# Stick-breaking attention: pairs of heads, worked inside the key and value loops, with fp32r cumulative sums

## What is computed

```python
def _sb_block(q_blk, k, v, q_pos):
    t_len = k.shape[2]
    k_pos = jnp.arange(t_len)
    z = jnp.einsum('bhqd,bhkd->bhqk', q_blk, k).astype(jnp.float32) * (SB_HEAD_DIM ** -0.5)
    causal = k_pos[None, :] < q_pos[:, None]
    log_keep = jnp.where(causal, -jax.nn.softplus(z), 0.0)
    after = lax.cumsum(log_keep, axis=3, reverse=True) - log_keep
    w = jnp.where(causal, jnp.exp(jax.nn.log_sigmoid(z) + after), 0.0)
    return jnp.einsum('bhqk,bhkd->bhqd', w.astype(v.dtype), v)

def stick_breaking_mixer(x, w_qkv, w_o):
    qkv = (x @ w_qkv).reshape(b, t_len, 3, SB_HEADS, SB_HEAD_DIM).transpose(2, 0, 3, 1, 4)
    q, k, v = qkv[0], qkv[1], qkv[2]
    ...
    return o @ w_o
```

## Time and profile before

| | |
|---|---|
| median of 3 runs | 1375.29 us (1373.15 to 1376.83) |
| span of the profiled execution | 1373.0 us (the lowest run, 1373.15, is next to it; the median lies 2.3 us above it) |
| PE busy | 1300.8 us, 95% |
| DVE busy | 851.3 us, 62% |
| ACT busy | 667.8 us, 49% |
| POOL busy | 36.4 us, 3% |
| mean granted clock of PE | 0.977 |
| key units | until 717.0 us |
| scores of heads 0 to 2 | 717.0 to 719.2 us |
| value units | 719.2 to 752.9 us |
| loop over heads | 752.9 to 818.7 us |

### The profile page before, as it was taken

One profiled execution on the slowest core, in us unless ns is written; L12 is line 12 of the kernel. 1 busy time (PEld: TensorE's weight loads), 2 busy tenths in 40 slices (PEclk: granted clock), 3 DMA queues, 4 the chain that ended last, 5 costly groups with the idle time before them and its releaser, 6 DMA issues.

```text
span 1373.0 us, 26931 instructions
## 1 busy us (share of the span) xinstructions
PE 1300.8 (95%) x10012; PEld 1251.6 (91%) x10012; DVE 851.3 (62%) x1246; ACT 667.8 (49%) x1015; POOL 36.4 (3%) x58
## 2 busy tenths in 40 slices
PE   5989999999998999999899999999999478999997
PEld 5989789999997999999899779999999478999997
DVE  3897675887555777754554536665446586666443
ACT  4453436646344666644343545565443455565331
POOL 1001210100000000000000000000000000000000
PEclk9999999999999999999999999999999688999999
DMA  4445333565443555555253104555554234455551
GB/s 165 139 153 170 108 105 106 160 214 168 138 138 116 161 185 184 185 190 185 82 170 107 31 1 152 169 171 181 171 177 128 79 113 146 153 172 179 171 177 51
DMA packets 56754, 197.44 MB, mean 144 GB/s; under 512 B 7136, under 2 KB 9440, under 8 KB 56560
## 3 DMA queue, kind: packets, MB, share of 16 engines
q1 hardware_dynamic: 54144, 194.01, 43.8%
q10 hardware_dynamic: 2544, 2.51, 0.6%
HBM read 195.45 MB, written 1.05 MB: 143 GB/s over the span
## 4 chain that ended last, share of the span: by engine, by line
PE 86%; DVE 9%; ACT 2%; issue 2%; DMA 1%; DVEq 0%; SPq 0%; ACTq 0%
PE acc L363 23%; PE acc L365 22%; PE acc L364 22%; PE mix L418 3%; DVE wlo L1132 2%; PE acc L401 2%; PE acc L402 2%; PE acc L403 2%; DVE xc L1320 1%; PE mix L481 1%; DVE uu L1596 1%; ACT whi L796 1%; PE mix L694 1%; PE mix L421 1%; DMA raw<-w 1%
## 5 line engine op out<-in xcount | busy, mean ns | idle before, releaser
L796 ACT ACTIVATE whi<-raw 128x1024 fp32r<-128x1024 f32 x368 | 388.1, 1058 | 516.2 <-PE acc L365 459.8
L1132 DVE TENSOR_TENSOR wlo<-raw,whi 128x1024 fp32r<-128x1024 f32 x368 | 449.5, 1223 | 245.6 <-ACT whi L796 245.3
L363 PE MATMUL acc<-xh,whi 128*128 128x256 f32 (+1 forms) x1664 | 481.4, 289 | 19.1 <-DVE xl L1139 14.9
L365 PE MATMUL acc<-xh,wlo 128*128 128x256 f32 (+1 forms) x1664 | 477.4, 287 | 0.0
L364 PE MATMUL acc<-xl,whi 128*128 128x256 f32 (+1 forms) x1664 | 477.0, 287 | 0.0
L363 PEld LDWEIGHTS acc<-xh,whi 128*128 128x128 f32 x1664 | 317.5, 191 | 23.6 <-DVE wlo L1132 20.2
L365 PEld LDWEIGHTS acc<-xh,wlo 128*128 128x128 f32 x1664 | 317.7, 191 | 0.0
L364 PEld LDWEIGHTS acc<-xl,whi 128*128 128x128 f32 x1664 | 316.7, 190 | 0.2
L365 PE MATMUL acc<-hh,wlo 128*128 128x272 f32 (+1 forms) x688 | 196.8, 286 | 0.0
L363 PE MATMUL acc<-hh,whi 128*128 128x272 f32 (+1 forms) x688 | 196.8, 286 | 0.0
L364 PE MATMUL acc<-hl,whi 128*128 128x272 f32 (+1 forms) x688 | 196.7, 286 | 0.0
(11 more groups left out here) (320 smaller groups left out, 1530.7 us busy)
## 6 DMA issues: line engine op xcount, KB each, us to landing
raw<-w SPq DMA_DIRECT2D x368, 512.0 KB, 3.5
hT<-xT ACTq DMA_DIRECT2D x1, 1024.0 KB, 10.3
mem<-memT ACTq DMA_DIRECT2D x1, 1024.0 KB, 5.4
out<-hT SPq DMA_DIRECT2D x8, 128.0 KB, 2.0
xdt<-wsmall ACTq DMA_DIRECT2D x1, 192.0 KB, 10.1
pr<-par ACTq DMA_DIRECT2D x1, 114.0 KB, 10.0
hT<-metaT ACTq DMA_DIRECT2D x1, 64.0 KB, 10.8
bcn<-wa ACTq DMA_DIRECT2D x1, 32.0 KB, 9.6
```

The costliest lines, as they stand in the source:

```text
L363: nc.tensor.matmul(dst, whi[:, slot, n, :], rh, start=first, stop=False)
L365: return nc.tensor.matmul(dst, wlo[:, slot, n, :], rh, start=False, stop=last)
L796: act.activation(whi[:, j, :, :].rearrange("p k c -> p (k c)"), raw[:, j, :], ACT.Copy)\
L1132: dve.tensor_tensor(wlo[:, j, :, :].rearrange("p k c -> p (k c)"), raw[:, j, :], whi[:, j, :, :].rearrange("p k c -> p (k c)").bitcast(F32 ...
```

## The change

- Heads go in pairs, `PAIRS` = 8, and all four `mix` banks hold scores, two pairs in turn. PE's stream is one loop over m = 0 to 10: `sb_after(m-3)`, then key unit m (m < 8) or value token pair m-8, then `sb_scores(m-1)`. Then `sb_out` of pairs 0 to 3, the last value token pair, `sb_out` of pairs 4 to 7, and `project("so")`.
- `sb_scores(p)` issues the three strips of both heads in turn, so that matmuls on rows 0 to 63 and on rows 64 to 127 alternate, then adds the causal mask in the bank: three bf16 matmuls per head, identity times `cmask` (0 and -1e30), of 128, 128 and 16 columns. `nmask` and `bmask` and their making on POOL are gone.
- The softplus: DVE sets the sign bit of the scores out of PSUM (`soft_abs`, in place of ACT's Abs and the scale -1), ACT does Exp and Ln, DVE adds max(z, 0) (`soft_sum`). ACT copies it into fp32r (`soft_hi`), DVE takes the rest (`soft_lo`); the multiplication by the mask is gone.
- `sb_after(p)` takes the sum over `softh` and then over `softl`, with `ntri` and `nones` (fp32r copies of tiles that now hold -1): 12 fp32r matmuls per head of the same sizes as the six before.
- ACT exponentiates straight out of PSUM into `wT`, which has a buffer for each of the 16 heads; DVE's min and mask step is gone.
- `sb_out(p)` alternates between the two heads of a pair (64 stationary columns each, PSUM partitions 0 to 63 and 64 to 127).
- At the program's start POOL makes `cmask`, `ntri` and `nones` besides the other constants.

On PE before, in the loop over heads (the sums of head 1, the output of head 0, the beginning of the scores of head 4): `lk` is the masked softplus, `tri` and `ones` the stationary tiles.

```diff
...
+        sp = sb("sp", [P, 2, ZC], stack=s4)
+        spt = sb("spt", [P, 2, ZC], stack=s4)
+        softh = sb("softh", [P, 4, ZC], F32R, stack=s4)
+        softl = sb("softl", [P, 4, ZC], F32R, stack=s4)
+        wT = sb("wT", [P, SBH, ZC], stack=s4)
...
-        zbank = [mix[:, 0, :], mix[:, 1, :], mix[:, 3, :], acc[:, 0, :]]
-        obank = [mix[:, 2, :], acc[:, 1, :]]
...
             pool.affine_select(out=bigm[:, :], in_=bigm[:, :], compare_op=ALU.is_ge, fill=BIG, base=0,
                                pattern=[[1, P]], channel_multiplier=-1).then_inc(consts, 1)
+            pool.affine_select(out=cmask[:, :], in_=cmask[:, :], compare_op=ALU.is_gt, fill=-BIG, base=0,
+                               pattern=[[1, P]], channel_multiplier=-1).then_inc(consts, 1)
+            pool.wait_ge(consts, CONSTS - 2)
+            for tile, exact in ((tri, ntri), (ones, nones)):
+                pool.tensor_copy(exact[:, :], tile[:, :]).then_inc(consts, 1)
...
-            project("sk", xh, xl, T2)
...
+            add = dict(start=False, skip_group_check=True)
+            def sb_scores(p):
+                pe.wait_ge(evacuated[p % 4], (OUTS["sk"] + p) // 4 + 1)
+                if p == 0:
+                    pe.wait_ge(sbmask, 1)
+                if p == 1:
+                    pe.wait_ge(misc_free, R["st_sb"] + 1)
+                if p >= 2:
+                    pe.wait_ge(wT_ready, 2 * p - 2)
+                both = [(64 * i, mix[:, 2 * (p % 2) + i, :]) for i in range(2)]
                 for t in range(3):
...
+                    for po, z in both:
+                        nc.tensor.matmul(z[:, at_c[t]:at_c[t] + T2 - at_q[t]], skT[po:po + 64, p, P * t:P * t + P],
+                                         sqT[po:po + 64, p, at_q[t]:T2], start=t == 0, stop=t == 2)
+                for po, z in both:
+                    nc.tensor.matmul(z[:, 0:P], identb[:, :], cmask[:, :], stop=False, **add)
+                    nc.tensor.matmul(z[:, T2:T2 + P], identb[:, :], cmask[:, :], stop=False, **add)
+                    nc.tensor.matmul(z[:, 2 * T2 - P:ZC], identb[:, :], cmask[:, 0:META], stop=True, **add)\
+                        .then_inc(head_ready, 1)
+            def sb_after(p):
+                for h in (2 * p, 2 * p + 1):
+                    z = mix[:, 2 * (p % 2) + h % 2, :]
+                    pe.wait_ge(softl_ready, h + 1)
+                    for n, part in enumerate((softh, softl)):
+                        l = part[:, h % 4, :]
+                        nc.tensor.matmul(z[:, 0:T2], ntri[:, :], l[:, 0:T2], stop=False, **add)
+                        nc.tensor.matmul(z[:, P:T2], nones[:, :], l[:, T2:2 * T2 - P], stop=False, **add)
+                        nc.tensor.matmul(z[:, 2 * P:T2], nones[0:META, :], l[0:META, 2 * T2 - P:ZC], stop=False, **add)
+                        nc.tensor.matmul(z[:, T2:2 * T2 - P], ntri[:, :], l[:, T2:2 * T2 - P], stop=False, **add)
+                        nc.tensor.matmul(z[:, T2 + P:2 * T2 - P], nones[0:META, :], l[0:META, 2 * T2 - P:ZC],
+                                         stop=False, **add)
+                        last = nc.tensor.matmul(z[:, 2 * T2 - P:ZC], ntri[0:META, :], l[0:META, 2 * T2 - P:ZC],
+                                                stop=n == 1, **add)
+                    last.then_inc(tri_ready, 1)
+            def sb_out(p):
+                if p == 0:
+                    pe.wait_ge(wT_ready, SBH)
+                if p >= 4:
+                    pe.wait_ge(yl_ready, 32 + p - 3)
+                for j in (0, 1):
+                    pe.wait_ge(evacuated[2 * (p // 2 % 2) + j], OUTS["sv"] // 4 + p // 4 + 1)
+                at_k = ((0, P, 0, T2), (P, P, T2, 2 * T2 - P), (2 * P, META, 2 * T2 - P, ZC))
+                for t, (q0, n, lo, hi) in enumerate(at_k):
+                    for h in (2 * p, 2 * p + 1):
+                        po = 64 * (h % 2)
+                        last = nc.tensor.matmul(mix[po:po + 64, p % 4, q0:T2], sv[0:n, t, 64 * h:64 * h + 64],
+                                                wT[0:n, h, lo:hi], start=t == 0, stop=t == 2)
+                last.then_inc(pv_done, 1)
+            for m in range(PAIRS + 3):
+                if m >= 3:
+                    sb_after(m - 3)
+                if m < PAIRS:
+                    unit("sk", m, m % 4, xh, xl, T2)
+                else:
+                    token_pair("sv", 2 * (m - PAIRS), xh, xl, tiles2)
+                if 1 <= m <= PAIRS:
+                    sb_scores(m - 1)
             for p in range(4):
...
+                sb_out(p)
+            token_pair("sv", 6, xh, xl, tiles2)
+            for p in range(4, PAIRS):
+                sb_out(p)
             project("so", yh, yl, T2, (yl_ready, 32))
...
-            units_loop("sk")
             HB = SSD_HEADS + XH
             exp_ln_tables()
...
+            def soft_terms(p):
+                for h in (2 * p, 2 * p + 1):
+                    t = sp[:, h % 2, :]
+                    act.wait_ge(sb_abs, h + 1)
+                    act.activation(t, t, ACT.Exp).then_inc(sb_act, 1)
+                    act.wait_ge(sb_act, 2 * h + 1)
+                    act.activation(t, t, ACT.Ln, bias=1.0).then_inc(sb_act, 1)
+            def soft_hi(h):
+                act.wait_ge(soft_ready, h + 1)
+                if h >= 4:
+                    act.wait_ge(tri_ready, h - 3)
+                act.activation(softh[:, h % 4, :], spt[:, h % 2, :], ACT.Copy).then_inc(softh_ready, 1)
+            def weights(h):
+                act.wait_ge(tri_ready, h + 1)
+                act.activation(wT[:, h, :], mix[:, h % 4, 0:ZC], ACT.Exp).then_inc(wT_ready, 1)
             def pair_out(p):
...
+                act.wait_ge(pv_done, p + 1)
+                act.activation(yh[:, p, :], mix[:, p % 4, 0:T2], ACT.Copy).then_inc(yh_ready, 1)
+            for m in range(PAIRS + 3):
+                p, q = m - 2, m - 3
+                if 0 <= p < PAIRS:
+                    soft_terms(p)
+                    soft_hi(2 * p)
+                if q >= 0:
+                    weights(2 * q)
+                if 0 <= p < PAIRS:
+                    soft_hi(2 * p + 1)
+                if q >= 0:
+                    weights(2 * q + 1)
+                if m < PAIRS:
+                    split_hi(UNITS["sk"][0] + m + 4)
+                else:
+                    split_hi(UNITS["sv"][0] + 2 * (m - PAIRS) + 4)
+                    split_hi(UNITS["sv"][0] + 2 * (m - PAIRS) + 5)
+            for p in range(4):
+                pair_out(p)
+            split_hi(UNITS["sv"][0] + 10)
+            split_hi(UNITS["sv"][0] + 11)
+            for p in range(4, PAIRS):
+                pair_out(p)
             units_loop("so", after_residual("so", "mlp0", T2))
...
-            units_loop("sk", scaled(skT, T2))
             HB = SSD_HEADS + XH
...
+            def soft_abs(h):
+                dve.wait_ge(head_ready, HB + h + 1)
+                dve.tensor_scalar(sp[:, h % 2, :].bitcast(U32), mix[:, h % 4, 0:ZC].bitcast(U32), SIGN, None,
+                                  ALU.bitwise_or).then_inc(sb_abs, 1)
+            def soft_sum(h):
+                dve.wait_ge(sb_act, 2 * h + 2)
+                dve.scalar_tensor_tensor(out=spt[:, h % 2, :], in0=mix[:, h % 4, 0:ZC], scalar=0.0,
+                                         in1=sp[:, h % 2, :], op0=ALU.max, op1=ALU.add).then_inc(soft_ready, 1)
+            def soft_lo(h):
+                dve.wait_ge(softh_ready, h + 1)
+                dve.tensor_tensor(softl[:, h % 4, :], spt[:, h % 2, :], softh[:, h % 4, :].bitcast(F32), ALU.subtract)\
+                    .then_inc(softl_ready, 1)
             def pair_lo(p):
                 dve.wait_ge(yh_ready, 32 + p + 1)
-                dve.tensor_tensor(yl[:, p, :], obank[p % 2][:, 0:T2], yh[:, p, :].bitcast(F32), ALU.subtract)\
+                dve.tensor_tensor(yl[:, p, :], mix[:, p % 4, 0:T2], yh[:, p, :].bitcast(F32), ALU.subtract)\
                     .then_inc(yl_ready, 1)
...
+            def values(m):
+                dve.wait_ge(unit_done, UNITS["sv"][0] + 2 * m + 2)
+                token_scaled(sv, 2 * m, (P, P, META))
+                split_lo(UNITS["sv"][0] + 2 * m + 4)
+                split_lo(UNITS["sv"][0] + 2 * m + 5)
+            for m in range(PAIRS + 3):
+                p = m - 2
+                if 0 <= p < PAIRS:
+                    for step in (soft_abs, soft_sum, soft_lo):
+                        step(2 * p)
+                        step(2 * p + 1)
+                if m < PAIRS:
+                    dve.wait_ge(unit_done, UNITS["sk"][0] + m + 1)
+                    dve.tensor_tensor(skT[:, m, 0:T2], acc[:, m % 4, 0:T2], rstd[:, :], ALU.mult)\
+                        .then_inc(evacuated[m % 4], 1)
+                    split_lo(UNITS["sk"][0] + m + 4)
+                else:
+                    values(m - PAIRS)
             for p in range(4):
...
+                pair_lo(p)
+            values(3)
+            for p in range(4, PAIRS):
+                pair_lo(p)
```

(16 more changed lines are left out.)

114 lines of the change are left out of this document (8 added, 106 removed).

## The result

The changed kernel takes **1381.93 us** (median of 4 runs, 1379.99 to 1382.92) against 1374.22 us for the kernel before (4 runs, 1372.31 to 1376.83): ratio 1.0052, 95% interval 1.0038 to 1.0067. The forecast was 1366.8 with a range of 1361 to 1381. The kernel is slower by 7.7 us where 8.5 us less was forecast. In the profiled execution (1379.99 us) the span is 1378.2 us against 1373.0, and the mean granted clock of PE is 0.963 against 0.977.

The account below looks back on a forecast made before the run. PE was taken to bound the kernel, the attention costing 68.0 us of it. Terms +2.6 - 6.4 + 2.9 - 8.7 + 1.1 = -8.5 us took 1375.3 to 1366.8 us, range 1361 to 1381.

Parts of the forecast that it names:

- A clock below 1.00 there: Sign that would prove the forecast wrong: PE's granted clock under 1.00 between the last query matmul and `so`; no chance given.
- Sums: Softplus sums on PE, one fp32r pass over high and low parts: 2.38 us a head against 2.21, +2.6 us.
- that rival: Narrow fp32r matmuls in the sums are dear: +12.8 us (1379.6), with double loads +22 (1389); chance 0.24.
- Scores: Scores on PE, two heads side by side in row halves: 1.03 us a pair, 9.0 against 15.4, -6.4 us.
- Masks: Causal masks, new on PE as bf16 matmuls: 0.36 us a pair with the uncovered load, 8 times, +2.9 us.
- Outputs: Attention outputs on PE, two heads of a pair side by side: 1.07 us a pair, 8.6 against 17.0, -8.7 us.
- Start: Pipeline's start: PE waits once for the softplus chain before the first sum, +1.1 us.
- At no cost: POOL's constants and removed masks, `split_lo` behind the softplus steps on DVE, SP's queue: claimed to add nothing.

Follow-up runs that it names:

- the first experiment: The changed kernel with its sums in plain float32 over the softplus itself, without high and low parts: 1364.8 us, ratio 0.9938.

## Why the prediction was wrong

**The step that failed** is in no part of the sum. It is the assumption under all of them that the clock stays at 1.00 because it is 1.00 in the earlier trace rows, where the loop over heads had sums of the same length. "A clock below 1.00 there" stood among the things that would make the prediction wrong, but neither in the rivals nor in the range. Priced from the rows: key units behind the sums 24.7 us against 16.1 with float32 sums, +8.6; value pairs 38.8 against 34.6, +4.2; sums 39.2 against eight pairs at 4.66, +1.9. Together 14.7 us. The forecast of -8.5 plus 14.7 gives +6.2; the table has +6.0, the spans +5.2, the medians +7.7.

Point by point:

1. **Sums**, 2.38 us a head forecast: 2.33 measured. The change costs 37.3 - 35.2 = +2.1 us at full clock where +2.6 was forecast. Narrow fp32r matmuls are not dear: L721, 16 by 16, steps in 0.13 us, and with full rows L718, 144 columns, in 0.07, so that rival falls. The arithmetic that halves the passes and doubles the parts was right. What it didn't ask is what the same 2.3 us do to the clock: by its own rate of 0.46 ns, the 608 columns of a part are 0.28 us of 1.17, and the rest is loads and changes of shape that a record still shows as busy.
2. **Scores**, 1.03 us a pair: measured 1.03. The two row halves run side by side, as the earlier trace rows let expect. The twelve passes, of 272 to 16 columns, start within 1.03 us, what six took before. The Trainium skill (TensorE: Matmul & The Clock Gate, "The mechanism") holds that matmuls start and end strictly in program order. By that, as the prediction worked it out, the time of a pair would have been 1.26; the trace has 1.03, and the measurement decides. But these rows show only passes out of order: the two heads' matmuls are issued in alternation, their first passes start at 748.751 and 748.758 and their second at 749.084 and 749.091, so each matmul as a whole still starts and ends in its turn. Whole matmuls out of order are in the kernel before, in the earlier trace rows and in the earlier trace rows, where a head's first 272 columns start at 717.576, ahead of a pass of 144 columns of the head before it at 717.693.
3. **Masks**, 0.36 us with the load: 0.29. Scores and masks are 1.32 us a pair.
4. **Outputs**, 1.07 us a pair: 4.30 for four pairs, 1.07.
5. **Start**, 1.1 us: one wait of 0.5 us by the list of waits, 0.6 by steps.
6. **At no cost**: right, no later wait of PE. The weights were forecast to be ready 0.2 us ahead at p = 2. With half of the sums PE waits for them for 0.4 us in all, and with the sign step moved for 0.5; the cover was about as thin as it was put.

At full clock, sums 37.3, scores with masks and wait 11.2 and outputs 8.6 are 57.1 us, 10.9 less than 68.0; the 2.2 us at the edges of the units, which the forecast had put into the scores' and the masks' price, make it -8.7 us against the forecast -8.5. (Two figures of the prediction don't follow from its rows and touch no term of the sum: the value units take 33.7 us, not 33.6, and 9.3 us of PE against 5.6 of ACT leave 3.7 us in a turn, not 2.) The sum was right, and the sign of the result was wrong.

**What the runs show of the cause.** The form of the sums is enough by itself: in the old loop, with stretches of about the same length, float32 sums read 1.00 and fp32r sums 0.50 throughout. In the new order the same form holds in half the length (high part only) and mostly holds when it is cut in two by weight matmuls, both from the second turn on. The float32 form holds at 4.39 us a pair and not at 8.8. Dense fp32r sums hold at 2.74 and not at 5.5. Both the form and the length of a stretch count, and so does what stands between two stretches. The order and the queues of the new pipeline are cleared by the first experiment, the steps of ACT and DVE by the high part alone.

**What stays open.** Between float32 sums of 4.39 us a pair, which held, and fp32r sums of 4.66, which did not, form and length both differ a little, and in the new order no run varied only one of them that finely. Why the clock falls in the first turn of the kernels with fp32r sums over 128 rows, high part only and sums cut in two is not settled either. All of these wait 0.5 us before the first sum, as the changed kernel does; in the three kernels of this pipeline without that wait (both with float32 sums of one part, and the one with the earlier sign steps) it didn't fall there. But no run changed the wait alone, and a wait of the same size elsewhere brought no fall. That the wait starts the falls of the changed kernel and the form of the sums only keeps them going is not ruled out by a run of its own; against the wait as the whole cause stand the old loop with fp32r sums, where the clock falls and PE waits for nobody, and the later turns of the high part alone and of the sums over 128 rows, where the wait has come before and the clock holds.

## What to carry to other kernels

An edit that makes a matmul cheaper per column but leaves its weight loads and shape changes in place makes a thin stretch, and PE at 100% busy can then lose half of its clock, for itself and for the dense work behind it. When an edit changes what PE does within a stretch that is granted 1.00, price a fall of the clock over the units behind as a rival of its own, and read the granted clock by stretch before believing any sum of durations. The cheaper cure was not arithmetic but shape: running a 16-row strip over all 128 rows, where the other rows hold zeros, took out the changes of shape, turned a change that cost 7.7 us into one that gains 24.5 (1350.0 against 1374.51), and gave the old kernel 7.8 us by itself.

## What the runs showed of the hardware that was not expected

- The granted clock falls without any idle time of PE in the trace: 0.50 over 100 us in which PE is busy for 100.00, and 0.64 over key units of 4.73 us which follow sums without a gap. The Trainium skill (TensorE: Matmul & The Clock Gate, "HAM oscillation — how this bites in real kernels") tells of the clock falling in waits for DMA, and its next section of short idle times between groups of matmuls. Here no wait or gap is in the records; whether they hide some within matmuls counted as busy, no run can tell.
- The slowdown can land behind its cause: in the two turns shown, scores and sums read 1.00, the unit behind them 0.64. In the first turns it took part of the sums as well.
- A strip of 16 rows is dearer than one of 128: 1.17 us a part with it, 0.68 without, though the array then has eight times the rows to work through. Timeline of PE in the kernel with the earlier sign step, one part over 128 rows, to be laid beside the turn at 750.07 above:

```profile
705.87 0.37 PE L717 MATMUL mix<-softh,ntri 128*128 128x272 f32 x1
706.08 0.23 PE L718 MATMUL mix<-softh,nones 128*128 128x144 f32 x1
706.15 0.22 PE L719 MATMUL mix<-softh,nones 128*128 128x16 f32 x1
706.22 0.32 PE L720 MATMUL mix<-softh,ntri 128*128 128x144 f32 x1
706.37 0.22 PE L721 MATMUL mix<-softh,nones 128*128 128x16 f32 x1
706.45 0.26 PE L723 MATMUL mix<-softh,ntri 128*128 128x16 f32 x1
706.56 0.37 PE L717 MATMUL mix<-softl,ntri 128*128 128x272 f32 x1
```

L718 steps in 0.07 us in place of 0.16, and L719 to L723 in 0.07, 0.15, 0.08 and 0.11 in place of 0.20, 0.27, 0.13 and 0.18: every step beside a change of shape shrinks.
